# The last expert block of a mixture-of-experts stage: which engine computes the remainders of the second product's weights

## The reference

```
def hierarchical_moe(h, w_group, b_group, w_expert, b_expert, w1, w3, w2):
    ...                      # each token goes to 2 of 32 experts
    xs = xf[tok]
    hid = jax.nn.silu(lax.ragged_dot(xs, w1, group_sizes)) * lax.ragged_dot(xs, w3, group_sizes)
    ys = lax.ragged_dot(hid.astype(xs.dtype), w2, group_sizes) * gate.reshape(-1)[order][:, None].astype(xs.dtype)
    return jax.ops.segment_sum(ys, tok, num_segments=n).reshape(B, T, D)
...
    x = x + gate2[:, None, :] * ffn.astype(x.dtype)
    return rmsnorm(x, final_norm_w)
```

## Time and profile before

| | |
|---|---|
| Median of 3 runs | 3309.79 us (3309.28 to 3310.51) |
| The profiled execution, its own time | 3308.52 us |
| Its span | 3306.7 us |
| TensorE, VectorE, ScalarE, GpSimd busy | 92%, 48%, 36%, 35% |
| Last matmul of the expert stage ends | 3252.44 us from the span's start |
| Last VectorE instruction | starts 3302.34 us, ends 3303.62 us |

### The profile page before, as it was taken

The page is one execution under the profiler, slowest core; times in us unless marked ns, Lnnn a source line. Parts: engine busy times, 40 slices in busy tenths (PEclk is TensorE's granted clock), DMA queues, the critical chain, the costliest instruction groups (busy, mean ns, idle before and its releaser), DMA issues. The chain is left out here.

```text
span 3306.7 us, 41072 instructions
## 1 busy us (share of the span) xinstructions
PE 3052.6 (92%) x14800; PEld 2257.2 (68%) x14800; DVE 1589.6 (48%) x2016; ACT 1184.7 (36%) x1702; POOL 1164.3 (35%) x597
## 2 busy tenths in 40 slices
PE   8999999989999989999899998999986899999992
PEld 5666666458888878874486557999544777777772
DVE  4444444431111111447544555446236777777774
ACT  3333333111111112221342222333213677777773
POOL 1100010213433434430033223224002777788874
PEclk9999999999999999999899999999987999999996
DMA  2000001211111122256300013001216999999995
GB/s 97 23 23 20 20 27 55 99 46 51 43 46 51 51 115 99 92 213 237 128 26 8 31 65 148 14 14 52 89 56 222 351 370 368 370 371 371 373 363 210
DMA packets 116293, 446.98 MB, mean 135 GB/s; under 512 B 14658, under 2 KB 15618, under 8 KB 111314
## 3 DMA queue, kind: packets, MB, share of 16 engines
q1 hardware_dynamic: 102740, 393.66, 32.1%
q0 software_dynamic: 7984, 28.66, 2.6%
q10 hardware_dynamic: 5456, 23.10, 1.7%
HBM read 401.18 MB, written 44.10 MB: 135 GB/s over the span
## 5 line engine op out<-in xcount | busy, mean ns | idle before, releaser
L3004 DVE TENSOR_TENSOR moe_w_low<-moe_raw_up,moe_w_high 128x1024 fp32r<-128x1024 f32 x288 | 436.3, 1553 | 156.4 <-ACT moe_w_high L2944 156.4
L2867 POOL TENSOR_TENSOR moe_w_low<-moe_raw_down,moe_w_high 128x1024 fp32r<-128x1024 f32 x144 | 417.2, 2929 | 148.8 <-ACT moe_w_high L2954 148.8
L2944 ACT ACTIVATE moe_w_high<-moe_raw_up 128x1024 fp32r<-128x1024 f32 x288 | 304.5, 1061 | 188.0 <-PE ps L2907 110.4
L91 PE MATMUL ps<-x1T_high,w_up_high 128*128 128x512 f32 x704 | 274.8, 390 | 3.5 <-PEq L3227 3.5
L91 PE MATMUL ps<-x1T_low,w_up_high 128*128 128x512 f32 x704 | 274.4, 390 | 0.0
L91 PE MATMUL ps<-x1T_high,w_up_low 128*128 128x512 f32 x704 | 274.3, 390 | 0.0
L2922 PE MATMUL ps<-moe_w_high,moe_x_high 128*128 128x512 f32 x576 | 229.3, 398 | 4.2 <-DVE moe_x_low L3035 4.2
L2924 PE MATMUL ps<-moe_w_high,moe_x_low 128*128 128x512 f32 x576 | 226.1, 392 | 0.0
L2923 PE MATMUL ps<-moe_w_low,moe_x_high 128*128 128x512 f32 x576 | 225.5, 392 | 0.0
L801 POOL TENSOR_TENSOR w_up_high<-w_up,consts 128x1024 fp32r<-128x1024 f32 x44 | 83.5, 1897 | 382.9 <-PE ps L91 285.3
L279 POOL TENSOR_TENSOR qkv_low<-qkv_raw,qkv_high 128x1024 fp32r<-128x1024 f32 x22 | 53.6, 2435 | 438.0 <-ACT qkv_high L578 438.0
(11 more groups left out here) (462 smaller groups left out, 6573.1 us busy)
## 6 DMA issues: line engine op xcount, KB each, us to landing
moe_raw_up<-in_w SPq DMA_DIRECT2D x288, 512.0 KB, 9.2
moe_raw_down<-in_w SPq DMA_DIRECT2D x144, 512.0 KB, 6.4
w_ada<-in_w_ada SPq DMA_DIRECT2D x48, 512.0 KB, 5.2
w_up<-in_ffn_w_up SPq DMA_DIRECT2D x22, 1024.0 KB, 4.8
w_down<-in_ffn_w_down SPq DMA_DIRECT2D x44, 512.0 KB, 3.4
y_rows<-xT ACTq DMA_DIRECT2D x36, 512.0 KB, 8.2
qkv_raw<-in_attn_w SPq DMA_DIRECT2D x22, 512.0 KB, 3.4
y_rows<-zero_rows SPq DMA_DIRECT2D x1, 8192.0 KB, 29.1
```

The lines of the kernel that those rows point to most:

```text
L91: ins = pe.matmul(out, stationary, moving, start=start and n == 0, stop=stop and n == last)
L2867: pool.tensor_tensor(w_low[:, down_slot(k)], raw_down[:, k], w_high[:, down_slot(k)].bitcast(F32), ALU.subtract).then_inc(down_low, 1)
L2944: act.activation(w_high[:, up_slot(n)], raw_up[:, n], ACT.Copy).then_inc(up_high, 1)
L3004: dve.tensor_tensor(w_low[:, up_slot(n)], raw_up[:, n], w_high[:, up_slot(n)].bitcast(F32), ALU.subtract).then_inc(up_low, 1)
```

## The change

After the loop, the remainders of pieces 1 and 3 of the last block's second product are computed by VectorE instead of GpSimd. GpSimd keeps pieces 0 and 2. VectorE's two instructions stand between `lower_hidden` and the two copy-outs, and they raise a new semaphore `last_low`; TensorE waits for `last_low` at pieces 1 and 3 and for `down_low` at pieces 0 and 2. The loop is unchanged.

```
+        LAST_ON_POOL, LAST_ON_VECTOR = [0, 2], [1, 3]
+        last_low = sem("moe_last_low")
...
-            def lower_down(b):
-                for k in range(HT):
+            def lower_down(b, pieces=range(HT)):
+                for k in pieces:
                     pool.wait_ge(down_high, 4 * b + k + 1)
...
-            lower_down(2 * last + 1)
+            lower_down(2 * last + 1, LAST_ON_POOL)
...
-            def multiply_down(b):
+            def multiply_down(b, end=False):
...
                 earlier(pe, y_out, NH * b)
                 for k in range(HT):
-                    pe.wait_ge(down_low, 4 * b + k + 1)
+                    if end and k in LAST_ON_VECTOR:
+                        pe.wait_ge(last_low, LAST_ON_VECTOR.index(k) + 1)
+                    elif end:
+                        pe.wait_ge(down_low, 4 * b + LAST_ON_POOL.index(k) + 1)
+                    else:
+                        pe.wait_ge(down_low, 4 * b + k + 1)
...
-            multiply_down(2 * last + 1)
+            multiply_down(2 * last + 1, end=True)
...
             lower_hidden(2 * last + 1)
+            for k in LAST_ON_VECTOR:
+                dve.wait_ge(down_high, 4 * (2 * last + 1) + k + 1)
+                dve.tensor_tensor(w_low[:, down_slot(k)], raw_down[:, k], w_high[:, down_slot(k)].bitcast(F32),
+                                  ALU.subtract).then_inc(last_low, 1)
             copy_out(2 * last, 0, last)
             copy_out(2 * last + 1, 1, last)
```

## The result

Median of 20 runs each: 3311.23 us before, 3315.97 us after. The ratio is 1.0014, with a 95% interval of 1.0008 to 1.0021, that is 2.6 to 7.0 us slower. The forecast was +5.0 us, which is 1.0015. The interval also holds the +2.7 us of rival 1, so what tells the two apart is the trace and not the time. The profiled execution's span went from 3306.7 to 3312.0 us.

What follows compares the result with a forecast made beforehand. The prediction took TensorE to bound the kernel, waiting in the tail for GpSimd's remainders. Later start +5.64, stop -0.71 and clock +0.1 made +5.0 us on 3309.79: 3314.8 us, range 3311.7 to 3316.6.

Steps and rivals of the forecast that it cites:

- rival 1: VectorE keeps its turn for both tail remainders instead of alternating with GpSimd: +2.7 us, 3312.5 us; chance 10%.
- What is removed: GpSimd's pieces 1 and 3 go, so TensorE loses its stop before the last piece: 0.7 us less.
- What is put in front of the copy-out: VectorE's two remainders delay the copy-out of the block before, which TensorE's first matmul awaits through `y_out`; no start at 3243.78.
- How long VectorE takes, and who goes next: In the tail VectorE and GpSimd alternate, held VectorE remainders ending 1.08 us after GpSimd's; TensorE starts 5.64 us later.
- Rival 2: The engines don't hold each other in the tail: +2.9 - 0.7 = +2.2 us, 3312.0 us; chance 3%.
- Rival 3: The copy-out doesn't bind TensorE's start in the tail, so only the stop goes: -0.7 us, 3309.1 us; chance 3%.
- The clock: TensorE restarts the tail at 1.2 GHz; a middle rise after 4.85 us adds 0.1 us, bounds -0.65 and +0.85.
- Rival 4: TensorE's clock rises only after the tail stage: 5.64 + 1.9 = +7.6 us, 3317.4 us; chance 6%.
- The sum: Tail total of later start, lost stop and clock: +5.64 - 0.71 + 0.1 = +5.0 us.
- its case alone: Tail start held by the copy-out with turns alternating: 3314.8 us, 3314.1 to 3315.7; chance 75%.

Runs made afterwards that it cites:

- Experiment 2: Changed kernel with the last block's second product in PSUM banks 0 and 1, without TensorE's wait on `y_out`: ratio 0.9998 to the kernel before.
- experiment 1: Changed kernel with VectorE's copy-out of the block before put back ahead of its two remainders: ratio 0.9998 to the kernel before.
- experiment 5: Kernel before plus one wait: VectorE's copy-out of the block before waits for the last block's fourth high part: 3315.33 us, a single run.
- experiment 6: Kernel before plus one wait: VectorE's copy-out of the block before waits for GpSimd's fourth remainder: ratio 1.0019 to the kernel before.
- experiment 4: Changed kernel with all four remainders on VectorE and the copy-out of the block before ahead of them: ratio 0.9995 to the kernel before.
- experiment 7: Changed kernel with all four remainders on VectorE and the copy-out ahead of the hidden remainder too: ratio 0.9989 to the kernel before.
- Experiment 8: All four remainders on VectorE, copy-out ahead of the hidden remainder, TensorE's high x high products first in the last block: ratio 0.9998 to the kernel before.

## Why the prediction was right

**What is removed.** Forecast 0.71 us for the stop. Experiment 2, at the same rise of the clock, gives 0.78.

**What is put in front of the copy-out.** This was the step that decided, and it holds: the one wait of TensorE is for the copy-out; with the order (1) or the banks (2) undone the loss is gone; with the gate alone (5, 6) it comes back without any work added.

**How long VectorE takes, and who goes next.** The forecast had VectorE's remainders at about 2.5 and 3.3 to 3.4 us, GpSimd's second at 3.3, and the start 5.64 us later. Measured were 2.54, 3.36, 3.31 and 5.64. The last figure is that exact by luck, since small errors cancel: GpSimd's piece 2 ended 2.20 us after VectorE, not 2.25, so that it and the copy-out behind it came 0.05 and 0.07 us earlier from H than forecast, and TensorE started 0.13 us after the copy-out's end, not 0.05. The 0.05 was read behind a GpSimd instruction; behind the copy-out it is 0.13 in the changed kernel and in experiments 5 and 6. The turns alternated, so rival 1, which had VectorE's second at 1.2 us, falls. Rival 2 (no holding) falls by the durations. By what the Trainium skill states (SBUF — State Buffer, "SBUF: two separate sides") an engine that starts first keeps the shared ports for the whole instruction, and the trace agrees: VectorE's held instructions end 1.08 us after GpSimd's, 0.13 us less than the 1.21 us that one takes alone. The 115 ns that the prediction takes from that section were measured there on a DMA whose descriptors GpSimd has to write. That the two take turns when both always have work, and that GpSimd's held instruction ends 2.20 to 2.24 us after VectorE's in these kernels and not 2.47 us, is from the traces.

**Rival 3**, that the copy-out doesn't bind TensorE, is what experiment 2 makes true: 0.8 us less than before, and only then.

**The clock.** Forecast was +0.1 us from a middle rise of 4.85 us; this execution had 6.06. Seven kernels run at the low clock from the first matmul on (in experiment 4 from 0.06 us after it) and have no stop; their stages line up with the rise: 7.30 us at a rise of 3.47, 7.88 at 4.65, 7.98 at 4.86, 8.01 at 4.86, 8.06 at 4.96, 8.19 at 5.23 and 8.58 at 6.06, that is (8.58 - 7.30) / (6.06 - 3.47) = 0.49 us for each microsecond at the low clock, where the prediction had 0.48. For the changed kernel this is +0.7 us against the kernel before. It is why the end came 5.56 us later and not 4.9. The term was too small by 0.6 us in this execution, although inside its bounds; that the changed kernel as such rises late is not shown, since it has one trace, and experiment 6, which starts later still, rose after 5.23 us. Rival 4, a clock low to the end of the stage, did not occur in any of the twelve profiled executions.

**The sum.** +5.64 (start) - 0.78 (stop) + 0.70 (clock) = +5.56 us in the profiled pair. With the clock's middle value the forecast of +5.0 stands, and the 20 runs of each put it at +4.7 in the medians. All of it reaches the time: from TensorE's end to the first gather it is 8.49 to 8.57 us, and to the end of the span 54.2 to 54.8 us, in all twelve profiled executions.

**The number itself.** The forecast was 3314.8 us, the median is 3315.97. The difference between the kernels was right; the base was not: the prediction built on a median of 3309.79 us from three runs, and over 20 runs it is 3311.23 us. The spread of 0.6 us either way that it took from the three was too small, as the 20 lie between 3309.11 and 3315.37 us. So the result is above the 3315.7 us of its case alone and inside the range of 3311.7 to 3316.6 by 0.6 us, only because that had been widened.

What stays open is the cause of the spread of the arrival at H (3239.1 to 3246.7). Most of it arises before the expert stage: the first high part of an up tile starts at 2518.1 us in experiment 1 and at 2526.6 in experiment 4. No run looked into it. Behind TensorE's end the spans differ by 0.6 us only, so this spread is likely what makes the intervals of the ratios so wide.

## What to carry to other kernels

Before putting work on an idle engine, list what stands behind it in that engine's queue and who waits for that: here VectorE was idle for 10 us, but the next thing in its queue freed the banks of TensorE's first matmul, and moving two lines below it turned a loss of 5.6 us into a gain of 0.6 in the tail. Then ask whether the second engine helps at all: two engines that hold each other out do not add up, and VectorE alone made four pieces (4.63 us) faster than two pieces beside GpSimd (5.82 us).

## What the runs showed of the hardware that was not expected

TensorE can restart at the high clock and lose it while busy. In experiment 7 it rested 3.06 us, the first matmul at 3243.88 ran at 2.4 GHz, and the granted clock fell to 1.2 GHz at about 3244.98 (0.99 in 3244 to 3245, 0.50 after), 1.1 us into the work, then rose again at 3248.4. So an earlier start does not save the stretch at the low clock, it moves it: the stage took 7.33 us there, against 7.30 in experiment 4, where the fall came 0.06 us after the first matmul. In both the clock was low for 3.4 us. Experiment 8 shows the same: idle for 1.71 us by its row, the fall 2.2 us after the start, and again 3.4 us at the low clock.

A rest of this length does not always end at the high clock, as far as the traces show. Counted from the end of TensorE's last transpose, the fall comes after 2.0 us in the kernel before (granted clock 0.81 in 3241 to 3242) and after 4.2 us in experiment 5 (0.89 in 3248 to 3249), with the same work ahead of it; the other executions lie between or at these. With a fall after 2.0 us, experiment 7 would have started at the low clock.

And two engines at turns keep a fixed rhythm: VectorE's held remainders took 2.54 and 3.36 to 3.39 us in all three kernels that share the pieces this way (the changed one, 1 and 2).
